# A two-block transformer in fp32 on one core: where panels and a modulation group stand in TensorE's order, and which waits its first tiles take

## The reference, cut to what matters

```python
h = rmsnorm(h_res, ln1_g); proj = h @ w_in
q, k  = latent queries and keys (8 heads of 96), RMS norm of each head, rotary part
out_a = softmax attention(q, k, v)                     # 8 latent heads
out_b = stick-breaking attention(sb_q, sb_k, sb_v)     # 8 heads of 64
out_c = softmax(q1 k1) v - lam * softmax(q2 k2) v, RMS norm   # 4 differential heads
merged = gate_a * (out_a @ wb_a) + gate_b * (out_b @ wb_b) + gate_c * (out_c @ wb_c)
h_res += merged @ w_out
h_res += square(relu(rmsnorm(h_res, ln2_g) @ w_ff1)) @ w_ff2
```

## Time and profile before

| what | value |
|---|---|
| median of 3 runs | 3295.46 us (3285.23 to 3296.98) |
| the profiled execution | 3289.24 us, span 3287.4 us |
| mean granted TensorE clock | 0.978 |
| TensorE matmul / weight load busy | 3170.4 us (96%) / 2675.2 us (81%) |
| VectorE, ScalarE, GpSimd busy | 1742.1 (53%), 1279.7 (39%), 1939.5 us (59%) |
| HBM traffic | 435.8 MB, 133 GB/s over the span |

### The profile page before, as it was taken

One profiled execution on the slowest core, in us unless ns is written; L12 is line 12 of the kernel. 1 busy time (PEld: TensorE's weight loads), 2 busy tenths in 40 slices (PEclk: granted clock), 3 DMA queues, 4 the chain that ended last, 5 costly groups with the idle time before them and its releaser, 6 DMA issues.

```text
span 3287.4 us, 48575 instructions
## 1 busy us (share of the span) xinstructions
PE 3170.4 (96%) x18046; PEld 2675.2 (81%) x18046; DVE 1742.1 (53%) x2425; ACT 1279.7 (39%) x2148; POOL 1939.5 (59%) x1285
## 2 busy tenths in 40 slices
PE   7999999999999999999999999999999999999999
PEld 6676899976768998888887777788887888886898
DVE  5564676655667766444334555544434443335554
ACT  3435555343555644222232343332223222235543
POOL 6657567705793974777657667578873786513000
PEclk9999999999989999999999999999999999999999
DMA  5322355532324664333434223344343434332354
GB/s 191 103 90 90 135 173 199 202 110 103 102 99 153 199 205 133 127 131 128 129 119 134 89 77 98 109 132 133 134 134 103 131 129 140 119 116 77 122 184 156
DMA packets 120280, 430.37 MB, mean 131 GB/s; under 512 B 13856, under 2 KB 17184, under 8 KB 119728
## 3 DMA queue, kind: packets, MB, share of 16 engines
q1 hardware_dynamic: 93632, 335.24, 30.7%
q0 software_dynamic: 24576, 86.46, 8.1%
q10 hardware_dynamic: 1904, 6.36, 0.5%
HBM read 426.95 MB, written 8.85 MB: 133 GB/s over the span
## 4 chain that ended last, share of the span: by engine, by line
PE 85%; POOL 5%; DVE 4%; ACT 2%; DMA 2%; issue 2%; ACTq 0%; DVEq 0%; SPq 0%; POOLq 0%
PE ps L481 21%; PE ps L483 21%; PE ps L482 21%; PE ps L508 2%; PE ps L578 2%; POOL macc L401 2%; PE ps L580 2%; PE ps L579 2%; DMA raw<-in_panels 2%; POOL modraw L399 1%; PE ps L522 1%; POOL mprod L399 1%; PE ps L523 1%; PE ps L527 1%; DVE wlo L1609 1%
## 5 line engine op out<-in xcount | busy, mean ns | idle before, releaser
L1609 DVE TENSOR_TENSOR wlo<-raw,whi 128x1024 fp32r<-128x1024 f32 x632 | 862.5, 1366 | 949.4 <-ACT whi L1050 922.7
L1050 ACT ACTIVATE whi<-raw 128x1024 fp32r<-128x1024 f32 x632 | 668.4, 1058 | 1436.5 <-PE ps L483 915.4
L481 PE MATMUL ps<-xhi,whi 128*128 128x512 f32 (+2 forms) x2784 | 946.8, 340 | 7.1 <-DVE wlo L1609 7.0
L483 PE MATMUL ps<-xhi,wlo 128*128 128x512 f32 (+2 forms) x2784 | 931.7, 335 | 0.0
L482 PE MATMUL ps<-xlo,whi 128*128 128x512 f32 (+2 forms) x2784 | 930.6, 334 | 0.0
L481 PEld LDWEIGHTS ps<-xhi,whi 128*128 128x128 f32 x2784 | 529.8, 190 | 76.9 <-issue 22.8
L482 PEld LDWEIGHTS ps<-xlo,whi 128*128 128x128 f32 x2784 | 530.0, 190 | 51.5 <-issue 1.9
L483 PEld LDWEIGHTS ps<-xhi,wlo 128*128 128x128 f32 x2784 | 529.5, 190 | 50.7
L399 POOL TENSOR_SCALAR modraw<-modraw,cs 128x512 f32<-128x512 f32 x288 | 548.0, 1903 | 27.6
L399 POOL TENSOR_SCALAR macc<-modraw,cs 128x512 f32<-128x512 f32 x36 | 73.9, 2052 | 809.0 <-PE ps L508 795.0
L399 POOL TENSOR_SCALAR mprod<-modraw,cs 128x512 f32<-128x512 f32 x252 | 449.0, 1782 | 19.0 <-POOL macc L401 0.2
(11 more groups left out here) (366 smaller groups left out, 4728.0 us busy)
## 6 DMA issues: line engine op xcount, KB each, us to landing
raw<-in_panels SPq DMA_DIRECT2D x632, 512.0 KB, 3.3
modraw<-in_mod POOLq DMA_DIRECT2D x144, 512.0 KB, 4.2
bias_by_column<-in_rpb POOLq DMA_DIRECT2D x16, 476.2 KB, 8.6
bia<-bias_by_column POOLq DMA_DIRECT2D x32, 96.0 KB, 2.6
rtab<-in_rtab ACTq DMA_DIRECT2D x2, 1312.0 KB, 8.0
wuq<-in_wuq ACTq DMA_DIRECT2D x2, 768.0 KB, 6.9
con<-in_con SPq DMA_DIRECT2D x1, 1345.5 KB, 13.7
h<-in_x SPq DMA_DIRECT2D x1, 1088.0 KB, 6.7
```

The costliest lines, as they stand in the source:

```text
L481: pe.matmul(out, w_hi, x_hi, start=start, stop=False)
L483: return pe.matmul(out, w_lo, x_hi, start=False, stop=stop)
L1050: act.activation(whi[:, s * PW:(s + 1) * PW], raw[:, s * PW:(s + 1) * PW], ACT.Copy).then_inc(hi_split, 1)
L1609: dve.tensor_tensor(wlo[:, s * PW:(s + 1) * PW], raw[:, s * PW:(s + 1) * PW], whi[:, s * PW:(s + 1) * PW].bitcast(F32), ALU.subtract).then ...
```

## The change

Five edits in one:

- `residual_tiles` with K = 8: the first two output tiles are computed together, six chunks of the one, six of the other, then the last two chunks of each; the waits for the input's low parts stand at the same chunks of the first tile.
- `residual_tiles` with larger K: the first product waits for K-4 low parts, and the last four are waited for one by one.
- `UNIT_FILL`: nine fillers at other units instead of eleven, and three panels instead of one after the last unit. The splits on VectorE for them stand after the spread heads 1, 4 and 7 instead of 3.
- `MOD_STICK` = (0, 7): the second modulation group of the stick heads follows the last head instead of the last but one, on all engines.
- Layer 0: two panels (`LEAD`) follow the first chunks instead of three, the third is the first of three whole tiles after it; its splits move from chunk 1 to 4 (ScalarE) and from chunk 2 to 5 (VectorE).

```diff
-MOD_UNIT, MOD_STICK = (6,), (0, 6)
+MOD_UNIT, MOD_STICK = (6,), (0, 7)
...
-UNIT_FILL = tuple(u for u in range(1, 22) if u % 2)
-UNIT_FILLS, SPREAD_FILL = len(UNIT_FILL) + 1, (4, 9, 14, 19)
+UNIT_FILL = (1, 3, 5, 7, 11, 15, 18, 20, 22)
+UNIT_FILLS, SPREAD_FILL = len(UNIT_FILL) + 3, (4, 9, 14, 19)
...
-                for m in range(NC):
+                if K == NC:
+                    pair = [(new_bank(), panel()) for _ in range(2)]
+                    for k0, k1 in ((0, K - 2), (K - 2, K)):
+                        for b, (wh, wl) in pair:
+                            for k in range(k0, k1):
+                                if b == pair[0][0] and k in (0, K - 2, K - 1):
+                                    lane.take(ready, 1 if k else K - 2)
+                                last = three(bank(b, 0, T), wh(k), wl(k), x_hi[:, k * w:k * w + T], x_lo[:, k * w:k * w + T], k == 0, k == K - 1)
+                            if k1 == K:
+                                last.then_inc(panel_done, 1)
+                for m in range(2 if K == NC else 0, NC):
                     b = new_bank()
                     for k in range(K):
-                        if m == 0 and ready is not None and k in (0, K - 2, K - 1):
+                        if m == 0 and ready is not None and (k == 0 or k >= K - 4):
 
-                            lane.take(ready, 1 if k else K - 2)
+                            lane.take(ready, 1 if k else K - 4)
...
-                first_tiles(T1, T1)
-                for _ in range(5 - FIRST):
+                lead = FIRST if layer else LEAD
+                first_tiles(T1, T1, lead)
+                for _ in range(5 - lead):
                     feature(T1)
...
-                elif c == 1:
+                elif c == 4:
                     split()
...
-                    if c == 2:
+                    if c == 5:
                         split()
...
-                    if j == 3:
-                        for n in range(len(UNIT_FILL), UNIT_FILLS):
-                            filler(n)
+                    if j in (1, 4, 7):
+                        filler(len(UNIT_FILL) + j // 3)
```

## The result

| | median us (lowest to highest, runs) | ratio to the kernel before, 95% interval |
|---|---|---|
| before | 3295.1 (3285.2 to 3297.7, 6) | |
| changed | 3269.4 (3258.9 to 3271.4, 6) | 0.9922 [0.9905, 0.9938] |

The changed kernel is 25.7 us faster where 31.9 were forecast; 3269.4 lies in the range. The profiled execution of it took 3271.4 us (span 3269.6), the longest of its six, so its trace shows only 17.8 us of gain.

A forecast was written before the change was run, and what follows sets the result against it. TensorE, busy 96% of the span, bounds the kernel, so only its idle time and lower-clock time can be won. Terms 3.6 + 15.3 + 7.5 + 0.6 + 4.9 = 31.9 us gave a 3264 us median, range 3250 to 3282.

The forecast's parts named there:

- Modulation after the last stick head: Stick heads, both layers: TensorE's wait for GpSimd's sum and the low clock behind it go; gain 15.3 us.
- Rival (3): Differential heads take the stick-head gain back through their ScalarE and VectorE chain: 15.3 us less, 3279; chance 0.06.
- Three panels behind the norms' sums: Head norms: two more panels cover the wait for inverse roots, with 0.6 us holes in units; gain 7.5 us.
- Two panels lead: Start of layer 0: first tile at 19.3, fourth panel's split ready under the third panel; gain 3.6 us.
- Finer waits: Second products of hidden layers and retention: "issue" waits are really for the low part and go; gain 4.9 us.
- Output tiles begin together: First residual output tiles: layer 1's 0.64 us wait inside the tile goes, the start stays; gain 0.6 us.
- Rival (2): The modulation wait moves along because GpSimd's group takes 60.7 us, and the clock loss comes with it: 3279; chance 0.08.
- Rival (1): The clock doesn't come back, low stretches turn up elsewhere: gain 18.5 us, 3277; chance 0.10.
- the rule behind it: Skill's rule that the clock's change point is run-variable: count idle time alone, not the forecast's 13.4 us of clock.
- Rival (5): Head units, thinned of fillers and with 0.6 us holes, fall to the lower clock: slower, 3322; chance 0.05.

The follow-up runs named there:

- e1_stick: Kernel before with only the second modulation group of the stick heads moved from behind head 6 to behind head 7: 3271.9 us, ratio 0.9937.
- e5_dummy: Kernel before plus seven fp32 products of no use in front of the modulation products behind stick head 6: 3280.6 us, ratio 0.9965.
- e9_norms: Changed kernel plus products of no use in front of three waits at each stage-ending norm: 3254.3 us, ratio 0.9888 to the kernel before.
- e6_threes: Changed kernel with head units' fillers spaced so at most three units follow one another without a panel: 3262.7 us, ratio 0.9927 to the kernel before.
- e12_all: Changed kernel plus useless products at norms, differential heads and output projections, fillers at most three units apart, VectorE's third split later: 3245.9 us, ratio 0.9863 to before.

## Why the prediction held, point by point

- **Modulation after the last stick head.** Right in every landmark: GpSimd in time, 7.8 and 8.0 us won against 7.6 and 7.7. The term was too small (15.3 against 20.7 alone, 16.1 to 25.3), and it is its clock part that was: 15.2 us by the means where I had counted 8.8, while the part at full clock is 5.6 for the 6.5 us of idle time. I had asked only for the clock up to the first differential transposes; with the group moved, the profile of e1_stick has 6.8 us at half clock from 300 to 640 and 13.6 from 900 to 1240, before 27.2 in each. That is 34 us, worth 17.
- **Rival (3), the differential heads take the gain back.** With the group alone moved they didn't: in e1_stick they took 35.9 and 35.8 us (before 37.3 and 36.3), and its four waits for the probabilities add up to 9.2 us, as before, in another split (3.98, 0.59, 4.00, 0.60). "Neither gain nor loss" held there. In the changed kernel's profile they took 42.6 us in layer 0 and 35.8 in layer 1, and the waits came to 11.4. The longer wait at the second head is not the moved group's own either: e5_dummy, whose group stays behind head 6, has 3.87 and 3.88 us there. The chain in front of it is VectorE's (2.47 and 2.35 us for its two scaling groups in the changed kernel, 1.49 and 3.07 in e5_dummy, 1.64 and 1.71 before), and the panel's split is only 0.7 us of it. GpSimd works beside it in all of these; see the last section.
- **Three panels behind the norms' sums.** The wait for the roots is gone and the holes are there as forecast (0.55 and 0.67). The units' stretch fell from 96.5 to 93.2 us in layer 0 (3.2 for 5.1) and grew from 93.7 to 94.9 in layer 1 (forecast 2.4 less), where the profile has the lower clock at 712 and 783. Alone the edit gave 5.6 for 7.5: the size of its clock share was off.
- **Two panels lead.** First tile right (19.49 for 19.3), fourth panel 1.5 us late. The mis-sized figure is 0.84 us a chunk on VectorE: with low parts of 1.24, 1.12 and 0.68 it was 1.1 on average (18.38 to 28.9 with the split's 1.4 taken out, over eight chunks). That left 2.1 us at the fourth panel, for 3.6. At the first head unit it is 4.3 on the mean of all profiles (80.4 against 84.7), because the old start also has later waits that differ from profile to profile. As a time it wasn't measurable.
- **Finer waits.** The mechanism was right: at none of the three products does TensorE wait, and "issue" was the low part. 4.2 at full clock for 4.9; alone, the ratio says 1.3, with an interval from 6 gained to 4 lost.
- **Output tiles begin together.** The wait of 0.64 us inside the tile is gone, the one at its start is 2.27 (2.22 before). It wasn't run alone, so its 0.6 us is read from the trace only.
- **Rival (2)** showed at another group than I had asked for: the one at the hidden layer of layer 1 waits 2.75 us for GpSimd (1.06 before) and takes 3.65 us instead of 1.97 behind it. But that isn't the shift of GpSimd's group that I had priced at nothing: GpSimd is idle for 44 us before this group, and in e1_stick, with the same shift, the wait is 0.79 us. GpSimd's group takes 60.9 us, as before (60.7), and TensorE comes 1.4 us sooner. The forecast had no term for a group that TensorE catches up with; it is some 3 us in this profile and in that of e9_norms (wait 2.81), and not in e6_threes (1.08) and e12_all (0.94).
- **Rival (1) and the rule behind it.** The saved clock did not go as a whole: 9.6 of 13.4. But the clock also fell where the diff changes nothing: the changed kernel's norm above is followed by PEclk 0.51, and the same place in the profile of before, with the same three waits, is at PEclk 1.00. So a single profile's low stretches say what such a stretch costs and not whether the next run has it. The Trainium skill, TensorE: Matmul & The Clock Gate, "What's actually happening", calls the point of the change run-variable; by that rule the two kernels' profiles could differ in the clock alone, and the trace agrees.
- **Rival (5), slower**, did not come: the units hold single short falls and no long one.

The terms add up to 31.9, the separate kernels to 20.7 + 5.6 + 1.3 - 0.3 = 27.3, the whole to 25.7. The total was near because the stick group gave more than its term and the small terms less: the mechanism was right, but that the errors cancelled is luck.

## What to carry to other kernels

Where an engine is busy for 97% of the span, price a wait by what the clock does behind it: here some 3 us of idle time were followed by up to 10 us at half clock, which is 5 us of time. Split every run's time into its part at full clock and the part lost to the clock before comparing kernels; edits worth under 5 us could only be seen in the first. Compare stretches of several profiles before you say that a gain was lost: a single one had luck of 3 to 4 us. And when a wait can't be removed, products of no use in it can be worth more than the edit that shortens it.

## What the runs showed of the hardware that was not expected

- Work added to TensorE's idle time made the kernel faster twice: by 11.5 us with 2 x 3.3 us of products, and from ratio 0.9922 to 0.9888 with about 2.3 us of products at each norm.
- Three waits of about 1 us each with small products between them (0.83, 0.99, 1.21) were followed by a stretch at PEclk 0.51 in the changed kernel's profile; no single long wait is needed. In the profile of before the same three waits were not.
- VectorE's same instruction takes 0.44 or 1.24 us (low part of a chunk) and three scalings 1.64 or 2.47, in stretches where GpSimd works. The Trainium skill, SBUF — State Buffer, "SBUF: two separate sides", has the port pair of the two as an exclusive lock; the traces agree. No run here stopped GpSimd, but the trace of before has stretches without it: from 1005 to 1059, where GpSimd is idle, all 15 panel splits of VectorE (line 1609, 128x1024) take 1.22 to 1.23 us; from 20 to 1000, where it is busy for 64%, they take up to 2.31. Over the whole trace the 224 splits with no GpSimd instruction beside them take 1.23 us at most, and the 357 with one for over half of their time up to 2.36. An instruction that reads one of its inputs from PSUM (line 2147, 128x512) takes 0.69 us both with GpSimd (48 of them) and without.
